# Norms, output projections and load order of a two-block transformer: token block by token block

## What is computed

```python
# first block
h = h + 0.5 * swiglu(rms_norm(h), ...)          # ffn_a
h = h + hybrid_mixer(rms_norm(h), ...)          # mixer: NSA heads and HGRN2 heads, then @ w_out
h = h + 0.5 * swiglu(rms_norm(h), ...)          # ffn_b
x = rms_norm(h)
# second block, twice: i = 0 (fox_mixer), i = 1 (mla_mixer)
x = layer_norm(ALPHA * x + 0.5 * swiglu(x))     # ffn_c / ffn_e
x = layer_norm(ALPHA * x + mixer(x))            # out projection fox_o / mla_o
x = layer_norm(ALPHA * x + 0.5 * swiglu(x))     # ffn_d / ffn_f
gate = sigmoid(x @ w_gate + b)                  # ple gate
x = layer_norm(ALPHA * x + gate * (p @ w_proj))
```

## Time and profile before

| | |
|---|---|
| median of 3 runs | 1881.82 us (1879.50 to 1884.51) |
| profiled execution | 1883.11 us, its span 1881.8 us |
| PE busy | 1748.9 us, 93% |
| DVE, ACT, POOL busy | 64%, 47%, 6% |
| mean granted PE clock | 0.96 |
| chain of work that ended last | PE 81%, DVE 9%, ACT 5% |
| PE, one 128x512 matmul to the next at full clock | 0.234 us |

### The profile page before, as it was taken

The page is one execution under the profiler, slowest core; times in us unless marked ns, Lnnn a source line. Parts: engine busy times, 40 slices in busy tenths (PEclk is TensorE's granted clock), DMA queues, the critical chain, the costliest instruction groups (busy, mean ns, idle before and its releaser), DMA issues.

```text
span 1881.8 us, 24791 instructions
## 1 busy us (share of the span) xinstructions
PE 1748.9 (93%) x9964; PEld 1508.4 (80%) x9964; DVE 1200.8 (64%) x1949; ACT 881.0 (47%) x1507; POOL 107.9 (6%) x147
## 2 busy tenths in 40 slices
PE   7999988689999999989999998899998998999985
PEld 6888887568888888888778887788887776888874
DVE  5766566746666666665756666576665554566655
ACT  4444445435444444455644444454444554454443
POOL 0000003321000000002110000100000000100000
PEclk9999997779999999999999999999998998999998
DMA  8544354004555554434435544255543222455521
GB/s 327 198 177 186 134 187 162 23 34 157 201 182 187 190 198 178 161 146 172 154 128 214 198 177 173 90 207 192 200 178 126 91 101 79 174 201 201 185 95 45
DMA packets 31954, 301.59 MB, mean 160 GB/s; under 512 B 3792, under 2 KB 4320, under 8 KB 5856
## 3 DMA queue, kind: packets, MB, share of 16 engines
q1 hardware_dynamic: 31840, 300.01, 43.2%
HBM read 298.93 MB, written 1.06 MB: 159 GB/s over the span
## 4 chain that ended last, share of the span: by engine, by line
PE 81%; DVE 9%; ACT 5%; issue 2%; POOL 2%; DMA 1%; SPq 0%; DVEq 0%; ACTq 0%; POOLq 0%
PE bank L388 29%; PE bank L378 24%; PE bank L377 10%; PE bank L367 8%; DVE w_lo L340 2%; ACT w_hi L333 2%; PE bank L380 1%; DVE x L630 1%; DVE x L654 1%; PE bank L1330 1%; POOL rstd L722 1%; PE bank L400 1%; PE bank L409 1%; PE bank L423 1%; PE bank L424 1%
## 5 line engine op out<-in xcount | busy, mean ns | idle before, releaser
L340 DVE TENSOR_TENSOR w_lo<-w_raw,w_hi 128x1024 fp32r<-128x1024 f32 (+5 forms) x545 | 607.6, 1167 | 280.3 <-ACT w_hi L333 279.7
L378 PE MATMUL bank<-xT,w_hi 128*128 128x512 f32 x1920 | 674.3, 396 | 1.2 <-DVE w_lo L340 1.2
L333 ACT ACTIVATE w_hi<-w_raw 128x1024 fp32r<-128x1024 f32 (+5 forms) x561 | 523.0, 993 | 173.8 <-PE bank L388 146.6
L377 PE MATMUL bank<-xT,w_lo 128*128 128x256 f32 x1680 | 468.5, 279 | 0.0
L378 PEld LDWEIGHTS bank<-xT,w_hi 128*128 128x128 f32 x1920 | 351.8, 188 | 71.3 <-DVE w_lo L340 1.9
L377 PEld LDWEIGHTS bank<-xT,w_lo 128*128 128x128 f32 x1680 | 316.9, 189 | 10.5
L588 ACT ACTIVATE ff_silu<-ff_silu 128x256 f32<-128x256 f32 x120 | 50.2, 419 | 390.7 <-DVE ff_silu L684 390.7
L388 PE MATMUL bank<-w_hi,hT_hi 128*128 128x512 f32 x528 | 206.1, 390 | 1.0 <-DVE hT_lo L693 1.0
L388 PE MATMUL bank<-w_hi,hT_lo 128*128 128x512 f32 x528 | 205.5, 389 | 0.0
L388 PE MATMUL bank<-w_lo,hT_hi 128*128 128x512 f32 x528 | 205.4, 389 | 0.0
L684 DVE TENSOR_REDUCE ff_silu<-bank 128x256 f32<-128x512 f32 x120 | 82.9, 691 | 111.4 <-PE bank L378 111.3
(11 more groups left out here) (320 smaller groups left out, 2327.5 us busy)
## 6 DMA issues: line engine op xcount, KB each, us to landing
w_raw<-in_ffn_a SPq DMA_DIRECT2D x22, 1536.0 KB, 6.6
w_raw<-in_ffn_b SPq DMA_DIRECT2D x22, 1536.0 KB, 6.6
w_raw<-in_ffn_c SPq DMA_DIRECT2D x22, 1536.0 KB, 6.5
w_raw<-in_ffn_d SPq DMA_DIRECT2D x22, 1536.0 KB, 6.7
w_raw<-in_ffn_e SPq DMA_DIRECT2D x22, 1536.0 KB, 6.5
w_raw<-in_ffn_f SPq DMA_DIRECT2D x22, 1536.0 KB, 6.5
gains<-in_gains SPq DMA_DIRECT2D x11, 1024.0 KB, 4.6
w_raw<-in_mla_up SPq DMA_DIRECT2D x8, 1280.0 KB, 5.7
```

The costliest lines, as they stand in the source:

```text
L333: nc.scalar.activation(hi, src, ACTF.Copy).then_inc(w_hi_made, 1)
L340: nc.vector.tensor_tensor(lo, src, hi.bitcast(F32), ALU.subtract).then_inc(w_lo_made, 1)
L377: nc.tensor.matmul(o[:, 0:SEQ], lo[:, c], xT[:, k, 0, :], start=False, stop=False)
L378: ins = nc.tensor.matmul(o, hi[:, c], xT[:, k, :, :], start=(k == 0), stop=(k == KD - 1))
```

## The change

1. **`pe_out`**: all chunks but the last two as before; then block 0 with the last two chunks, then block 1 with both. The last but one frees its pair only after block 1. The k-order of each accumulation is unchanged.
2. **Norms 2, 5, 7, 9** (`BY_BLOCKS`): the pieces come as (0, 0), (0, 1), (1, 0), (1, 1). The first products need three pieces. `pe_warm` issues 0, 0, 13 (10 at norm 2), 0 matmuls ahead of them instead of 13 (10, 42 at norm 7, 20 at norm 9), 3, 2, 0. ACT: squares of block 0, the split of the next ffn's first chunk (pieces 0 to 3), two turns, squares of block 1, two turns. DVE: add, mean, two applies for block 0; add of block 1; two lows; mean, two applies, two lows for block 1. POOL: root of block 0, its four pieces of `w_lo`, root of block 1. At norm 7 the add is the gated one, with the sigmoid of block 1 behind ACT's split. Before, the split and POOL's pieces stood ahead of the norm.
3. **Norm 11**: by block, and the output is written by two transfers of 0.5 MB (one for each block) instead of one of 1 MB.
4. **The mixer's order**: loads hg_fq 0, 1, cmp 0, hg_fq 2, cmp 1, hg_fq 3, cmp 2, hg_v 0, cmp 3, hg_v 1, nsa_b, nsa_c; PE's projections and compression matmuls in this order, with other PSUM banks. ACT: the copies of the compression sums and the split of nsa_b stand ahead of the logarithms, decays(1) stands where w_out1's first split stood. DVE: right(0) ahead of away(1). A third buffer for the decays (the raw slot of w_out1, used by head 2) joins the two; head 3 takes the first again.
5. **The unit loop**: ACT splits w_out1's first chunk in step 0, decays(2), (3) in steps 1 and 2. DVE, between `weights(k)` and `gated_weights(k)`: right(1) at k = 0, the low part of w_out1 and away(2) at 1, away(3) at 2, right(2) at 3, right(3) at 5; `mask_levels` ahead of `gated_weights`. ACT: the high part of the output ahead of its exponentials. POOL: left(2), (3) in steps 2 and 3. SP loads ffn_b's second chunk behind one more wait (for the raw slot that the decays borrow) and asks for a further step of the loop ahead of `load_gains(2)`.

The core of the diff:

```diff
+    behind_cmp = {("hg_fq", 2): 0, ("hg_fq", 3): 1, ("hg_v", 0): 2, ("hg_v", 1): 3}
...
+BY_BLOCKS = (2, 5, 7, 9)
...
         def pe_turn(n, src, pieces=range(4)):
             for p in pieces:
-                b, k0 = p % 2, p // 2 * 4
-                bank = psum[4 + 2 * b + p // 2]
-                pe_warm(({7: 42, 9: 20}.get(n, 13 if n >= 4 else 10), 3, 2, 0)[p])
+                b, half = piece_of(n, p)
+                k0, bank = 4 * half, psum[4 + 2 * b + half]
+                pe_warm(((0, 0, 13 if n >= 4 else 10, 0) if n in BY_BLOCKS else (13 if n >= 4 else 10, 3, 2, 0))[p])
                 pe.wait_ge(normed, 4 * n + p + 1)
...
         def pe_out(names, a_hi, a_lo, k_tiles, per, signal=None):
 
             todo = [first[name] + i for name in names for i in range(t[name].shape[0])]
-            for c, i in enumerate(todo):
+            last = len(todo) - 1
+
+            turns = [(c, b) for c in range(max(last - 1, 0)) for b in range(TB)]
+            turns += [(c, b) for b in range(TB) for c in range(max(last - 1, 0), last + 1)]
+            for c, b in turns:
+                i = todo[c]
                 wait_split(pe, i)
                 ks = list(range(c * per, min(c * per + per, k_tiles)))
-                for b in range(TB):
-                    for half in range(2):
-                        ins = token_major(psum[2 * b + half][:, :], w_hi[chunks[i].pair], w_lo[chunks[i].pair],
-                                          lambda j: D * j + 512 * half, 512, ks, a_hi, a_lo, b, c == 0, i == todo[-1])
-                        if i == todo[-1]:
-                            ins.then_inc(signal or acc_made, 1)
-                if i != todo[-1]:
+                for half in range(2):
+                    ins = token_major(psum[2 * b + half][:, :], w_hi[chunks[i].pair], w_lo[chunks[i].pair],
+                                      lambda j: D * j + 512 * half, 512, ks, a_hi, a_lo, b, c == 0, c == last)
+                    if c == last:
+                        ins.then_inc(signal or acc_made, 1)
+                if c != last and b == TB - 1:
                     ins.then_inc(out_used, 1)
...
+        def act_norm_blocks(n, ffn):
+
+            mean = n >= 4
+            act_squares(n, x, mean, (0,))
+            act_split(first[ffn], 0, 4)
+            act_turn(n, (0, 1))
+            act_squares(n, x, mean, (1,))
+            act_turn(n, (2, 3))
...
+        def dve_turn_blocks(n, add, apply, eps):
+
+            add(0)
+            dve_mean(n, 0, eps)
+            for half in range(2):
+                apply(n, 0, half_of(half))
+            add(1)
+            dve_low(n, 0)
+            dve_low(n, 1)
+            dve_mean(n, 1, eps)
+            for half in range(2):
+                apply(n, 1, half_of(half))
+            dve_low(n, 2)
+            dve_low(n, 3)
...
+        gains_lent = gains[:, 0:LEVELS * SEQ]
         decayed = [a.rearrange("p (l s) -> p l s", l=LEVELS) for a in (
-            gains[:, 0:LEVELS * SEQ], logs[:, :, :, :].rearrange("p a h s -> p (a h s)"))]
+            gains_lent, logs[:, :, :, :].rearrange("p a h s -> p (a h s)"),
+            raw[chunks[first["w_out1"]].slot][:, 0:LEVELS * SEQ], gains_lent)]
...
+            pe_features(place["hg_fq", 0], [(bank(2), (nsa_copied, 3)), (bank(3), (nsa_copied, 4))], mix_tile)
+            pe_features(place["hg_fq", 1], [(bank(4), (nsa_copied, 5)), (bank(5), (gate_made_hg, 1))], mix_tile)
+            compressed(0)
+            pe_features(place["hg_fq", 2], [(bank(6), (gate_made_hg, 2)), (bank(7), (gate_made_hg, 3))], mix_tile)
+            compressed(1)
+            pe_features(place["hg_fq", 3], [(bank(0), (gate_made_hg, 4)), (bank(2), (fk_sig_made, 1))], mix_tile)
+            compressed(2)
+            pe_tokens(place["hg_v", 0], SEQ, [(bank(3), (q_made, 1)), (bank(4), (fk_sig_made, 2))], mix_tile)
+            compressed(3)
+            pe_tokens(place["hg_v", 1], SEQ, [(bank(5), (q_made, 2)), (bank(6), (fk_sig_made, 3))], mix_tile)
+            pe_features(first["nsa_b"], [(bank(7), (q_made, 3)), (bank(0), (fk_sig_made, 4)), (bank(2), (q_made, 4))], mix_tile)
             pe.wait_ge(part_made, 2)
...
+            act.wait_ge(hid_tile, 4)
+            for kv in range(2):
+                nc.scalar.activation(part[kv], psum[1][:, kv * CMP_HID:(kv + 1) * CMP_HID], ACTF.Copy).then_inc(part_made, 1)
+            act_split(first["nsa_b"])
...
+                if k == 0:
+                    act_split(first["w_out1"])
+                if k in (1, 2):
+                    decays(k + 1)
...
+                m, b = decayed[h], b_sum[:, h, :]
+                if h == 2:
+
+                    wait_split(dve, first["w_out1"])
+                if h == 3:
+
+                    dve.wait_ge(gram_made, 4)
+                    dve.wait_ge(cross_made, 1)
...
             away(0)
-            dve_split(first["nsa_b"])
+            dve_split(first["nsa_c"])
+            right(0)
             away(1)
-            right(0)
-            dve_split(first["nsa_c"])
-            right(1)
-            dve_split(first["w_out1"])
...
+                if k == 0:
+                    right(1)
+                elif k == 1:
+                    dve_split(first["w_out1"])
+                    away(2)
+                elif k == 2:
+                    away(3)
+                elif k in (3, 5):
+                    right(2 + k // 5)
                 if k < STEPS:
+                    mask_levels(k)
                     gated_weights(k)
-                    mask_levels(k)
                 if k >= 2:
                     output_lo(k - 2)
-                if k in (2, 4):
-                    away(1 + k // 2)
-                if k in (3, 5):
-                    right(1 + k // 2)
             dve_split(first["w_out1"] + 1)
             dve_split(first["w_out2"])
 
...
+                if k in (2, 3):
+                    left(k)
...
+            loads(RAW_SLOTS, first["ffn_b"] + 1)
 
             sp.wait_ge(gram_made, 12)
             sp.wait_ge(cross_made, 3)
+            loads(first["ffn_b"] + 1, first["ffn_b"] + 2)
+            sp.wait_ge(gram_made, 16)
+            sp.wait_ge(cross_made, 4)
...
-            sp.wait_ge(normed, 46)
-            nc.sync.dma_start(out.rearrange("(b p) d -> p b d", p=P), x[:, :, :]).then_inc(out_landed, 16)
-            sp.wait_ge(out_landed, 16)
+            for b in range(TB):
+                sp.wait_ge(normed, 45 + b)
+                nc.sync.dma_start(out[tok_of(b), :], x[:, b, :]).then_inc(out_landed, 16)
+            sp.wait_ge(out_landed, 16 * TB)
...
-            act_squares(2, x, False)
-            act_turn(2)
+            act_norm_blocks(2, "ffn_b")
...
+        def pool_norm_blocks(n, ffn):
+            pool_root(n, (0,))
+            split_lo_pool(first[ffn])
+            pool_root(n, (1,))
```

More of the change, by code:

```diff
@@ L163, in cuts, with take @@
         return (0, cols // 4 * 2, cols)
-    chunks, first = [], {}
-    for name in ("ffn_a", "nsa_a", "nsa_v", "hg_g", "hg_fq", "hg_v", "cmp_w1", "nsa_b", "nsa_c", "w_out1", "w_out2",
+    chunks, first, place = [], {}, {}
+    def take(name, i):
+        n, _, cols = t[name].shape
+        by_pool = 4 if i == 0 and name in ("ffn_b", "ffn_d", "ffn_e", "ffn_f") else 0
+        place[name, i] = len(chunks)
+        first.setdefault(name, len(chunks))
+        chunks.append(Chunk(name, t[name][i, :, :], cols, cuts(name, i, cols) if name != "cmp_w1" else (), by_pool, i))
+    behind_cmp = {("hg_fq", 2): 0, ("hg_fq", 3): 1, ("hg_v", 0): 2, ("hg_v", 1): 3}
+    for name in ("ffn_a", "nsa_a", "nsa_v", "hg_g", "hg_fq", "hg_v", "nsa_b", "nsa_c", "w_out1", "w_out2",
                  "ffn_b", "ffn_c", "fox_f", "fox_v", "fox_qk", "fox_o1", "fox_o2", "ffn_d", "ple0_p",
@@ L169, in weight_stream @@
                  "ffn_f", "ple1_p", "ple1_g1", "ple1_g2"):
-        first[name] = len(chunks)
-        n, _, cols = t[name].shape
-        for i in range(n):
-            split = cuts(name, i, cols) if name != "cmp_w1" else ()
-            by_pool = 4 if i == 0 and name in ("ffn_b", "ffn_d", "ffn_e", "ffn_f") else 0
-            chunks.append(Chunk(name, t[name][i, :, :], cols, split, by_pool))
+        for i in range(t[name].shape[0]):
+            if (name, i) in behind_cmp:
+                take("cmp_w1", behind_cmp[name, i])
+            take(name, i)
             chunks[-1].packed = name in ("ffn_a", "ffn_b") and i == FF_TILES - 1
@@ L209, in weight_stream @@
         c.hi_at[j], c.lo_at[j], c.pool_at[j] = hi, lo, pool
-    return chunks, first
+    return chunks, first, place
 FFN = ("ffn_a", "ffn_b", "ffn_c", "ffn_d", "ffn_e", "ffn_f")
 FFN_NORM = (1, 3, 4, 6, 8, 10)
+BY_BLOCKS = (2, 5, 7, 9)
 N_TURNED = 11
@@ L227, in build @@
         pe, act, dve, pool, sp = (Line(e) for e in (nc.tensor, nc.scalar, nc.vector, nc.gpsimd, nc.sync))
-        chunks, first = weight_stream(t)
+        chunks, first, place = weight_stream(t)
         w_landed = [sem(f"w_landed_{i}") for i in range(RAW_SLOTS)]
@@ L296, in freed @@
```

(34 more changed lines are left out.)

176 lines of the change are left out of this document (73 added, 103 removed).

## The result

The changed kernel takes 1869.39 us in the median of its runs (1861.84 to 1870.51) beside 1881.69 for the kernel before: a ratio of 0.9925 with an interval of 0.9896 to 0.9955. Two later batches of runs gave 0.9958 (0.9946 to 0.9971, 11 runs) and 0.9937 (0.9922 to 0.9953): the change is worth 8 to 14 us.

What follows compares the result with a forecast made beforehand. PE, the matmul engine, bounds the kernel with 81% of the chain, so only its idle or half-clock places give time back. 1883.1 - 10 - 1.5 - 9 + 4 - 1.7 = 1864.9, 1864 in the median; range 1850 to 1881.

Steps and rivals of the forecast that it cites:

- The projections: Mixer's projections: the new load order closes PE's 9.1 us wait and the half clock behind it; gain 10 us.
- The start of the loop: Ahead of the scores: one decay exponential (1.91 us) replaces ACT's 2.85 us split, shortening PE's 2.6 us wait; gain 1.5.
- The loop: Unit loop: work moved into DVE's 2.51 us waits takes eight steps from 89 to 75 us; less PE's clock, gain 9.
- the forecast's first seven steps: Unit loop, k=0 to k=6: predicted step times 8, 12, 10, 11, 8.5, 9.5 and 8 us.
- the 5 us taken for PE's clock: Unit loop: PE idle over 4 us in k=1, then half clock over k=2, k=3 and part of k=4; costs about 5.
- the lock: Norms: two-SBUF-input DVE and SBUF-reading GpSimd instructions exclude each other; applies and gated adds could wait for a 1.26 us piece.
- The norms: Norms 2, 5, 7, 9: blockwise work -6.8 to +6 us, taken +1; half-clock stretches 3; in all +4, from -7 to +16.
- The step of POOL's queue: Norm 2: POOL's four pieces end 2.8 us later, block 1's root behind them 2.0 later; 0.3 net loss.
- The end: Last norm and output: shorter path 0.6 us, half-size last transfer 1 to 1.5; taken 1.7, from 0.5 to 3.
- Rival (b): Loop not shortened, half clock at k=1, steps near 13 us; only nsa_b's hole and the end gained: 1873, chance 0.25.
- Rival (c): PE at 0.50 clock through the loop, eight steps of 13 us, norms +16: 1900, slower; chance 0.09.
- What would show it: Signs: 9.1 us wait under 2, full clock up to 308, score steps 68 us for 80, no 3.8 us root waits.

Runs made afterwards that it cites:

- copies_first: The changed kernel with decays(1) behind, not ahead of, the copies of the compressed keys and values: 1869.9 us, 0.9933 of the kernel before.
- after_again: The changed kernel, unchanged, run and traced again: 1872.33 us, 0.9958 of the kernel before.
- swap_masks: The changed kernel with gated_weights(k) put back ahead of mask_levels(k), as before the change: 1865.58 us, 0.9921 of the kernel before.
- warm: The changed kernel with more warm matmuls ahead of the pieces of norms 2, 5, 7, 9: 1865.19 us, 0.9922 of the kernel before.
- pool_tiny: The changed kernel with POOL's four low-half pieces cut to 8 of 512 columns, the rest left out: 1861.79 us, 0.9892 of the kernel before.
- mixer_end: The kernel before with parts 3, 4 and 5, and decays(1) behind the copies; old norms 2, 5, 7, 9 and output projections: 1862.61 us, 0.9903.
- out_old: The changed kernel with the output projection's old order, norms still by block: 1888.12 us, 1.0037 of the kernel before.
- after_third: The changed kernel, unchanged, run and traced a third time: 1869.43 us, 0.9937 of the kernel before.

## Why the prediction was right, and where its steps were not

The forecast was 1864 with a range of 1850 to 1881, faster at 0.78; 1869.4 is in the range, 5 us above the point.

**The projections (forecast 10).** Right in mechanism and nearly in size: nsa_c starts 78.5 us behind the mixer's first product where it started 87.95, 9.4 earlier. The new lateness came one chunk later than I looked for it: 0.98 us ahead of nsa_c, whose low half DVE makes behind away(0).

**The start of the loop (forecast 1.5).** Wrong in sign, by about 3, and the one step that failed outright: the wait is 3.1 for 2.6, and the first score step is 7.9 earlier where 9.4 + 1.5 was due. The step that failed is "one decay exponential stands there (1.91 us)"; the table load of 1.28 belongs to it, and copies_first shows the two moved away. The scores themselves ran at half clock behind that hole (the first four matmuls, L912 now and L856 before, took 2.04 for 1.18).

**The loop (forecast 14 less 5 for the clock, 9).** The net came out at 6.2 from the first to the last score step. The reason given was wrong in part: for the most part it wasn't PE's clock but DVE's own work. From step 1 to 2, 13.7 us against the 12 of the forecast, DVE has no wait above 0.3 us while PE runs at half clock beside it:

```profile
312.00:326.00 14.00, 13.52 (x51) 10.79 (x52) 13.79 (x48) 6.83 (x24) 3.32 (x4) 0.51 0.01 2
```

DVE is busy 13.79 of 14.0 us, but PE is too, 13.52, so this trace alone leaves both. after_again settles it: the step took the same 13.7 there, 310.35 to 324.05, with PE at full clock and a quarter idle from 314.5 on:

```profile
314.50:324.05 9.55, 6.96 (x46) 5.51 (x46) 9.38 (x30) 4.52 (x13) 2.78 (x3) 1.00 0.00 1
```

The term missing is the 1.8 us of DVE's time in each step by which mask_levels, put first, lets POOL's sums run beside gated_weights. With it out (swap_masks) first to last score step is 69.4, near the 67 to which the forecast's first seven steps add up, although step 4 grows from 8.7 to 11.1. I had read the order of the two as free. Of the 5 us taken for PE's clock some 2 are seen, in step 5: it took 11.7 with 6.8 us at half clock in the changed kernel, and 9.7 with none in warm. The forecast named the lock, with its rule from the Trainium skill's page SBUF — State Buffer (Who interferes with whom), at the norms, and didn't look for it here, where the same rule bears: the gated weights have both inputs in SBUF, and the sums on POOL read SBUF.

**The norms (forecast +4, from -7 to +16).** +2 to +6 in the traces, so right. Of its terms: the gaps changed by -0.9 to -0.2 in all, where I had +1; the half-clock stretches cost 2.9 to 6.4 where I had 3. The lock costs 5.4 of gaps (pool_tiny); without it the change's own gain is 6.3, near the 6.8 taken for the end of the range. The step of POOL's queue was right in size, in part by luck. At norm 2 the four pieces end 3.0 us behind the last matmul's end (417.61), as forecast, and the root of block 1 starts at 3.2; but it finds POOL idle, by 0.2 us:

```profile
415.62 5.01 POOL L357 TENSOR_TENSOR w_lo<-w_raw,w_hi 128x512 fp32r<-128x512 f32 x4 [2.50 <-ACT w_hi L343]
420.85 0.55 POOL L767 TENSOR_TENSOR rstd<-rstd,minus_half 128x1 f32<-128x1 f32 x1 [0.21 <-DVE rstd L651]
```

Chain of norm 2 in the changed kernel:

```profile
417.61 0.45 PE bank L427 x4
418.08 1.09 ACT xT L582 x2
419.17 1.23 ACT xn L568 x4
420.42 0.16 DVE rstd L649
...
420.85 0.56 POOL rstd L767
421.43 0.76 DVE xn L674
```

ACT copies block 0's two turned pieces ahead of squaring block 1; that ended last, 0.2 us behind the pieces of w_lo, and stands where block 0's apply stood. With POOL's pieces all but gone (pool_tiny) the gap of norm 2 is the same 6.36.

**The end (forecast 1.7).** 1.4 behind the last transfer (4.05, now 2.66; 2.6 to 2.7 in all nine kernels with two transfers), and 1.5 ahead of it (from PE's last product to that transfer 13.1, now 11.6): right in direction, 2.9 in all, at the upper bound of its 0.5 to 3. The forecast didn't say that the second part hangs on the projection's new order; with the old one (mixer_end, out_old) this stretch is 15.6, longer than before.

```profile
1857.84 0.34 SPq L1998 DMA_DIRECT2D out<-x  x1
```

**The sum.** Mixer -12.7 (the two traces with the old order and the three of the changed kernel: 224.3 in the mean before, 211.6 after), norms +3.4 (66.5 in the mean for 63.1), end -2.9: about -12, and 12.3 was measured. The forecast had -20.5, +4 and -1.7: what is missing is the mixer's, 3 us at the loop's start and 3 in the loop; the rest lies behind the last score step, where the traces differ among themselves. Rival (b), 1873 with the loop not shortened, was the nearest to the second batch's 1872.3, but by another cause. Rival (c), half clock through the loop, did not come: 33 to 37 us of the loop's 82 ran at 0.50, where it had been 46 of 89. What would show it: the 9.1 wait is under 2, the 3.8 waits for POOL's root are 1.0, and no new wait for the weights of hg_fq or hg_v has come. The 68 us of score steps didn't come (74.0); nor did the full clock ahead of the loop, as PE is at 0.50 from 295.1, at the scores; nor, in this trace, half clock behind norm 2, which after_third has.

## What to carry to other kernels

Before work is moved in the order of one engine, look at what it releases on the engines that share a port with it: here a swap of two steps that cost nothing by count cost 14 us of DVE's time in eight steps and 4 us of the kernel's, and no wait shows it, only longer busy times of tiny operations. A norm or a reduction done by halves gains only if its helpers stay out of its way and if the matmul engine's hole behind it stays filled: at norms 5 and 9, 23 instead of 13 filling matmuls, with like ones at 2 and 7, took 4.4 us out of the norms, and so filled the by-block norms were even with the old ones. And a single trace of one execution is not the kernel: untouched stages differed by 3 to 6 us.

## What was not expected of the hardware

Two executions of the same instructions differed by 6 us by PE's clock alone: holes of 1 to 3 us at the loop's tail were followed by some 20 us at 0.50 in one trace and by none in another. And an operation of one column (0.16 us) took 0.94 beside POOL's pieces: three products of two columns each took 1.38 us beside its sums for 0.30.
